# Moving two 64 KB tensors of a hybrid decoder layer from the bottom of SBUF to its top

## The reference

```python
h_in = rms_norm(x, pre_mix_norm_w)
proj = h_in @ w_in                      # 1024 -> q, k, v, o, gates, conv_val, conv_gate
qk = silu(causal_depthwise_conv(qk_raw, qk_conv_w, qk_conv_b))
h_tilde = mlstm_chunkwise(q, k, v_raw, i_pre, f_pre)      # 4 heads x 128, chunks of 128
y_mlstm = sigmoid(o_pre) * layer_norm_per_head(h_tilde) * mlstm_norm_w
u = causal_depthwise_conv(conv_val * sigmoid(conv_gate), conv_w, conv_b)   # width 31
y_conv = silu(layer_norm_per_group(u) * conv_norm_w + conv_norm_b)
x = x + rms_norm(concat([y_mlstm, y_conv]) @ w_out, post_mix_norm_w)
h2 = rms_norm(x, pre_mlp_norm_w)
a = relu(h2 @ w_ff1)                    # 1024 -> 4096
x = x + rms_norm((a * a) @ w_ff2, post_mlp_norm_w)
```

## Time and profile before

| | |
|---|---|
| median of 3 runs | 2515.39 us (2514.12 to 2517.88) |
| the profiled execution's span | 2515.5 us (this execution is the one the rows are of) |
| TensorE busy | 2337.6 us, 93% of the span |
| VectorE, ScalarE, GpSimd busy | 1500.7 us (60%), 781.5 us (31%), 176.1 us (7%) |
| mean granted TensorE clock | 0.960 |
| moved by DMA | 212.72 MB, mean 85 GB/s |

### The profile page before, as it was taken

How to read it: one execution, slowest core, us unless ns; L and a number is a source line. 1 busy time by engine, 2 the same in 40 slices (tenths; PEclk the granted TensorE clock), 3 DMA queues, 4 the chain that set the end, 5 groups by cost and what they waited for, 6 DMA issues and landing times.

```text
span 2515.5 us, 30415 instructions
## 1 busy us (share of the span) xinstructions
PE 2337.6 (93%) x10945; PEld 1927.5 (77%) x10945; DVE 1500.7 (60%) x2366; ACT 781.5 (31%) x1604; POOL 176.1 (7%) x96
## 2 busy tenths in 40 slices
PE   6899999999687777699999999999999999999997
PEld 3688879789566666578888888888788888888886
DVE  6899999790455555435454555545755455554546
ACT  5323333233334333432222223222432222223122
POOL 4111211111000000000000000000300000000003
PEclk8999999999888888899999999999999999999999
DMA  4111112022646666661111111113611111111113
GB/s 169 31 45 63 63 59 84 26 79 73 183 114 172 165 155 157 166 223 44 57 42 50 50 50 42 42 58 114 224 63 42 58 42 50 42 55 45 42 33 109
DMA packets 144452, 212.72 MB, mean 85 GB/s; under 512 B 7568, under 2 KB 97808, under 8 KB 144368
## 3 DMA queue, kind: packets, MB, share of 16 engines
q1 hardware_dynamic: 132016, 190.44, 25.2%
q10 hardware_dynamic: 12224, 21.04, 2.2%
q0 software_dynamic: 128, 0.13, 0.0%
HBM read 156.93 MB, written 54.66 MB: 84 GB/s over the span
## 4 chain that ended last, share of the span: by engine, by line
PE 48%; issue 29%; DMA 10%; DVE 8%; SPq 3%; ACT 1%; POOL 1%; POOLq 0%; DVEq 0%; ACTq 0%
PE psum L1446 14%; PE psum L1466 13%; PE psum L332 11%; DMA winter_b<-scratch_rows 9%; PE psum L322 6%; DVE c_buf L590 2%; SPq L897 1%; PE psum L336 1%; DMA big_lo<-scratch_h_lo 1%; PE psum L1010 1%; DVE qout L602 1%; SPq L899 1%; POOL acc L1428 1%; DVE big_lo L546 1%; DVE big_raw L551 1%
## 5 line engine op out<-in xcount | busy, mean ns | idle before, releaser
L1576 DVE TENSOR_TENSOR acc<-acc,psum 128x512 f32<-128x512 f32 x480 | 326.4, 687 | 221.4 <-PE psum L1466 218.5
L1446 PE MATMUL psum<-big_hi,w_hi 128*128 128x512 f32 x1024 | 406.6, 397 | 9.5 <-DMA big_lo<-scratch_h_lo 9.5
L1446 PE MATMUL psum<-big_hi,w_lo 128*128 128x512 f32 x1024 | 406.1, 397 | 0.0
L1446 PE MATMUL psum<-big_lo,w_hi 128*128 128x512 f32 x1024 | 406.0, 396 | 0.0
L1466 PE MATMUL psum<-w_hi,hid_hi 128*128 128x512 f32 x1024 | 399.8, 390 | 3.6 <-issue 3.6
L1466 PE MATMUL psum<-w_lo,hid_hi 128*128 128x512 f32 x1024 | 399.7, 390 | 0.0
L1466 PE MATMUL psum<-w_hi,hid_lo 128*128 128x512 f32 x1024 | 399.4, 390 | 0.0
L590 DVE SCALAR_TENSOR_TENSOR c_buf<-u_buf,par_a,c_buf 128x1024 f32<-128x1024 f32 x240 | 342.7, 1430 | 8.5 <-ACT c_buf L440 1.3
L1564 DVE TENSOR_TENSOR sq<-relu 128x512 f32<-128x512 f32 x128 | 90.8, 709 | 346.0 <-ACT relu L1499 346.0
L1446 PEld LDWEIGHTS psum<-big_hi,w_hi 128*128 128x128 f32 x1024 | 193.4, 189 | 56.8 <-issue 5.5
L1446 PEld LDWEIGHTS psum<-big_lo,w_hi 128*128 128x128 f32 x1024 | 193.5, 189 | 46.8
(11 more groups left out here) (196 smaller groups left out, 3631.4 us busy)
## 6 DMA issues: line engine op xcount, KB each, us to landing
w_raw<-in_w SPq DMA_DIRECT2D x128, 512.0 KB, 3.6
w_raw<-in_w_in SPq DMA_DIRECT2D x25, 512.0 KB, 4.1
scratch_qk<-qout ACTq DMA_DIRECT2D x16, 512.0 KB, 2.6
x_c<-in_x SPq DMA_DIRECT2D x16, 512.0 KB, 4.2
scratch_xn<-xn SPq DMA_DIRECT2D x16, 512.0 KB, 5.2
scratch_h_hi<-h_hi SPq DMA_DIRECT2D x16, 512.0 KB, 15.7
scratch_h_lo<-h_lo SPq DMA_DIRECT2D x16, 512.0 KB, 15.4
big_hi<-scratch_h_hi SPq DMA_DIRECT2D x4, 2048.0 KB, 15.1
```

Of the source, the lines that this page charges most:

```text
L1446: mm = nc.tensor.matmul(psum[:, tb, :], l, r, start=kt == 0 and i == 0, stop=kt == KT - 1 and i == 2)
L1576: nc.vector.tensor_tensor(out, out, psum[:, 2 + j % 4, :], ALU.add).then_inc(sem["acc"], 1)
```

## The change

The two tensors of the kept part, `big_lo` (with `big_raw` in the same bytes) and `big_hi`, get fixed addresses at the top of SBUF. They are moved nowhere in time: what is in them, when it is written and who reads it stays as it is. Everything that was laid behind them moves down by 65,536 bytes. In phase C the tensors are also laid in another order. No instruction is added, removed or moved on any engine, and no wait is changed: the five engines' instructions with their waits are the same rows in the same order, so the change has no rows of the order to show.

```diff
+BIG_AT = 163712
...
         acc = sb("acc", [P, NT, D])
-        w2_hi = sb("w2_hi", [P, 2, D], F32R)
+        xn = sb("xn_c", [P, Q_RING, D])
+        w2_raw = sb("w2_raw", [P, 2, D])
         w2_lo = sb("w2_lo", [P, 2, D], F32R)
-        w2_raw = sb("w2_raw", [P, 2, D])
-        xn = sb("xn_c", [P, Q_RING, D])
         junk = sq[:].rearrange("p a b -> p (a b)")
 
+        sb("behind_phase_b", [P, 8])
         w1_hi = sb("w1_hi", [P, 2, KT, P], F32R)
...
         wpost = sb("wpost_c", [P, D])
+        w2_hi = sb("w2_hi", [P, 2, D], F32R)
...
-    with nc.sbuf_tensor("big_raw", [P, KT, D], F32) as raw:
-        pass
-    big = {"raw": raw, "lo": sb("big_lo", [P, KT, D], F32R), "hi": sb("big_hi", [P, KT, D], F32R)}
+    def top(name, dt, half):
+        return nc.alloc_sbuf_tensor_at(name, [P, KT, D], dt, offset=BIG_AT + half * KT * D * 4)
+
+    big = {"raw": top("big_raw", F32, 0), "lo": top("big_lo", F32R, 0), "hi": top("big_hi", F32R, 1)}
```

## The result

The changed kernel takes 2537.45 us (median of 6 runs, 2535.24 to 2542.06); the kernel before takes 2518.68 us, the median of its six executions, or 2517.88 us of the five that are left without a slow one of 2957.99 us. The ratio of the kernels is 1.0085, 95% interval 1.0075 to 1.0096: slower by about 21 us (19 to 24), where 21 us less were forecast. The profiled execution spans 2538.4 us against 2515.5 us. A time is 1.7 to 1.9 us longer than the span of the same execution (here 2540.2 against 2538.4 us), so the span of 2515.5 us isn't an execution of 2515.39 us, and the closeness of those two numbers is chance; these 2 us are too small to touch the argument.

The account below looks back on a forecast made before the run. TensorE's matmul stream was taken to bound phase C, TensorE and then VectorE phase A, broadcast loads phase B. Terms -19.8 - 1.0 - 0.3 = -21.1 us against 2515.5 us gave 2494 us, range 2481 to 2510 us.

Parts of the forecast that it names:

- The first product, -19.8 us: Phase C, L1446: moving big to the top takes blocks from 22.39 to 21.77 us, 32 x 0.62 us saved.
- comparison 2: Phase A, one weight tensor: tokens moving from big 232.7 ns per matmul, from h_hi1 and h_lo1 227.4; put down to place.
- Comparison 1: Phase C blocks: 22.39 us for L1446 moving low-lying big, 21.77 us for L1466 moving high-lying w2; read as place's price.
- Comparison 3: Phase A, L322, 256 columns: stationary tokens low on big 116.7 ns, high 119.8 ns; a low stationary operand saves 3.1 ns.
- The second product, 0: Phase C, L1466: w2_hi, w2_lo and hid move; ends +6.6 and -9.5 us, taken as 0, blocks staying at 21.77 us.
- worst case: Phase C, L1466: w2_lo's new, unknown place has at worst big's old price, +6.6 us.
- first rival: Phase C, L1466: hid's low stationary place pays off with 512 columns too, -9.5 us more, 2484.5 us; chance 0.22.
- Phase A, -1.0 us: Phase A: L332 gains 4.3 us, L322 loses 2.4 us, half counted because VectorE is close behind.
- Phase B, -0.3 us: Phase B, L1010 moving w_out: loads hide most matmuls, 48 at the end on the chain gain 6.4 ns each.
- the place does nothing: Whole kernel: the two distances come from something else going with these tensors; time stays 2515.5 us; chance 0.09.
- The slower one: Phase C: distance between operands costs; L1466 turns slow, +19.8 us, L1446 gains a third, -6.6 us; 2529 us; chance 0.05.
- the distance rule: Matmul operands: it is the distance between moving and stationary operand that costs, not the place, with a limit between 57,000 and 76,000 bytes.

Follow-up runs that it names:

- e1: Kernel before with 128 unused bytes in front of big and 384 behind it; ratio 0.9925 against the kernel before.
- e2: Changed kernel with 192 unused bytes in front of w2_hi, putting it at 0 modulo 256; ratio 1.0006 against the kernel before.
- e9: Kernel before with 64 unused bytes in front of w2_hi and 192 between w2_hi and w2_lo, so only w2_hi's low bits change; ratio 1.0057.
- e6: Kernel before, padded: first product's moving operand 16 bytes behind the stationary one modulo 256, second's 224; one execution, +15 us.
- e4: Changed kernel, big at the top, every operand of the three-matmul products at 0 modulo 256; 2497.43 us, ratio 0.990 against the kernel before.
- e3: Kernel before, big at the bottom, padded so every operand of the three-matmul products starts at 0 modulo 256; 2496.83 us, ratio 0.990.
- e10: Kernel before, padded: first product's moving operand 4 bytes ahead of the stationary one modulo 256, second's 192 behind; one execution, 0 us difference.
- e8: Kernel before, padded: first product's moving operand 224 bytes behind modulo 256, in the second only w2_lo 64 off; one execution, +11 us.

## Why the prediction was wrong

The view of what bounds the kernel held: phase C is TensorE's stream, and nothing but the distance of starts changed. So did the unit price (the second product rose by 0.63 us per block; I had a price of 0.62 us for the opposite effect) and, but for two, the count of 32 blocks. The sign is the failure, and it has two steps.

- **The first product, -19.8 us: measured 0** (22.39 to 22.40 us). The step that failed is comparison 2, "what differs is the place". Two slots with one weight tensor differ in place and also in their start modulo 256 (128 for big, 160 for the other half and the weights). I took the table of addresses by thousands of bytes and didn't look at its low bits. Comparison 1 fits both readings in the same way. e1 separates them: 128 bytes bring 0.63 us per block and some 19 us in all. Comparison 3 falls with it: L323 on big, now at the top, kept its 116.7 ns, so that the low place of a stationary operand never was what saved the 3.1 ns.
- **The second product, 0: measured +18 us.** I wrote that w2_hi moves "hardly (to 152,640)". These 8128 bytes leave it at 64 modulo 256 beside hid at 0; e2 and e9 show that this is the loss: e2 takes all of it away, and e9 brings 14 us of the 21 (9 to 20). For the operand that moved least I had asked for no price. My worst case, +6.6 us for w2_lo, stood on the wrong tensor, and the low stationary operand's saving (first rival) did not come: hid at the bottom with agreement gives 21.82 us (e2).
- **Phase A, -1.0 us: 0.** Every tensor there moved by a multiple of 256, so L333 and L323 kept their distances to 0.4 ns. TensorE's wait for the taps stayed at 2.9 us, 3.0 before; the chain enters the o slots 0.8 us later than before.
- **Phase B, -0.3 us.** From that entry to the load before phase C the profiled execution is 3.7 us longer than before. No rival priced it and no run ties it to the change: e1 reaches this load at 1062.68 us and e2 at 1066.14 us, with other layouts. The loads set this phase, and over the thirteen traces, each of another layout, the load before phase C begins anywhere from 1057.69 us (before) to 1066.90 us (e6). How much of that is the layout and how much the single execution is open.

The rivals: "the place does nothing" (0.09) was right about the place, but not about the kernel, since I had made it mean no change. The slower one (0.05, 2529 us) named the right product with the right size, L1466 at 22.4 us, for a wrong reason: by the distance rule the first product had to gain a third in the same run, and e4 has the same distances as the changed kernel within a few hundred bytes and is 24 us quicker than before. What I had said would prove me wrong altogether, "L1446 still at 22.39 us", is what came.

The two pages of the Trainium skill that I set against the change (SBUF — State Buffer, "Who interferes with whom"; TensorE: Matmul & The Clock Gate, "Back-to-back issue gap") have no term for an address. For high and low addresses the traces agree with that. For the low bits they don't: 226.7 and 233.2 ns for one shape at one granted clock (1.00), with nothing but 128 bytes between them (e1). The distance of some 216 ns that I quoted is, in that section, the gap of an isolated matmul; its figure for a sustained stream, some 131 ns, is still farther from the 226.7 ns that were the least here. That TensorE never waits on another engine is not touched by it.

## What to carry to other kernels

When two streams of the same matmul run at two rates, compare everything in which they differ, down to the low bits of the operands' addresses, before giving the difference a name; a shift by a few hundred unused bytes is the cheap test. Lay float32r operands that meet in a matmul of 512 columns so that they start at the same address modulo 256 (here worth 1% of the kernel for some 600 bytes per partition, e3), and check this again whenever a tensor is claimed in front of them, since every tensor behind it moves. A layout change without a change in the program is not neutral.

## What the hardware showed that I had not expected

- A stream of float32r matmuls of 128x512 runs at 226.7 ns per matmul (21.76 us for 96) or, at another offset of the two operands modulo 256, at up to 236.6 ns (22.71 us, moving operand 4 bytes behind).
- The price is no matter of agreement alone: beside a stationary operand at 0, 4 bytes ahead is free, 64 bytes behind nearly so (21.97 us), and with 256 columns the offset of 32 bytes is quicker than agreement (116.7 against 119.8 ns). With 64 bytes, a mixture of offsets in the cycle of three matmuls costs more than a uniform one (22.27 and 22.40 against 21.97 us). One pair of starts can run at two rhythms: 227 and 232 ns in e10, 229 and 233 ns in e8.
- The mechanism stays open. The runs show that the two addresses act on the rate, not what in the chip waits; that both operands are read at the same time and meet somewhere would fit, but was only thought of, not tried. Offsets between those of the table, and other types than float32r, were not tried either.
